# The first half of an output projection spread over six attention heads, and their probabilities turned by VectorE and a DRAM round

## The reference

```
u = rmsnorm(h, norm_g[l])
p = u @ w_in[l]                       # 1024 -> 9216 columns
hq, hf_f, hf_b, hi, hgt, aq, ak, av, agt = split(p)
o_h = hgrn2_mixer(...)                # 8 heads, gated linear recurrence in both directions
o_a = diff_attention_mixer(...)       # 8 heads
h = h + concat(o_h, o_a) @ w_out[l]   # 2048 -> 1024
```

```
s = einsum('bqhcd,bkhcd->bhcqk', q, k) * scale     # c = 0, 1: the two components, 64 wide
p = softmax(s)
p_diff = p[:, :, 0] - lam * p[:, :, 1]
o = einsum('bhqk,bkhv->bqhv', p_diff, v)           # v is 128 wide
o = rmsnorm(o, subln_g) * (1 - lam_init) * silu(gate)
```

## Time and profile before

| | |
|---|---|
| three runs, median | 1385.91 us |
| the profiled execution, its own time | 1386.22 us |
| its span | 1384.4 us |
| PE busy | 1369.9 us, 99% |
| DVE busy | 1046.2 us, 76% |
| ACT busy | 837.3 us, 60% |
| POOL busy | 186.0 us, 13% |
| DMA, share of 16 engines | 33.0% |
| granted TensorE clock | 9 tenths or more in all 40 slices |

### The profile page before, as it was taken

How to read it: one execution, slowest core, us unless ns; L and a number is a source line. 1 busy time by engine, 2 the same in 40 slices (tenths; PEclk the granted TensorE clock), 3 DMA queues, 4 the chain that set the end, 5 groups by cost and what they waited for, 6 DMA issues and landing times.

```text
span 1384.4 us, 32303 instructions
## 1 busy us (share of the span) xinstructions
PE 1369.9 (99%) x13108; PEld 1291.0 (93%) x13108; DVE 1046.2 (76%) x1765; ACT 837.3 (60%) x1802; POOL 186.0 (13%) x158
## 2 busy tenths in 40 slices
PE   9999999999999999999999999999999999999998
PEld 9999999998999999999998888888888899999987
DVE  6888887788646777877667888888886478888864
ACT  7666666666434666666555667666664456666654
POOL 1111222220000000000001122222210000000100
PEclk9999999999999999999999999999999999999999
DMA  5332322332323333333233232333323233334432
GB/s 188 117 98 93 108 85 86 108 108 78 99 71 122 101 99 100 103 90 100 70 107 108 87 106 85 108 107 108 108 82 108 85 110 107 108 107 114 114 96 76
DMA packets 76340, 140.41 MB, mean 101 GB/s; under 512 B 9504, under 2 KB 39456, under 8 KB 76192
## 3 DMA queue, kind: packets, MB, share of 16 engines
q1 hardware_dynamic: 76192, 138.35, 33.0%
HBM read 112.36 MB, written 17.30 MB: 94 GB/s over the span
## 4 chain that ended last, share of the span: by engine, by line
PE 89%; DVE 5%; ACT 2%; issue 2%; DMA 0%; SPq 0%; DVEq 0%; ACTq 0%
PE proj L1926 64%; PE far L2191 5%; PE pair L2174 3%; PE pair L2176 3%; PE far L2208 2%; PE pair L2059 1%; PE far L2193 1%; PE far L2144 1%; PE far L2145 1%; PE pair L2124 1%; DVE ops L1660 1%; PE pair L1926 1%; PE pair L2131 1%; DVE w_lo L1392 1%; PE far L2148 1%
## 5 line engine op out<-in xcount | busy, mean ns | idle before, releaser
L1926 PE MATMUL proj<-u_hi,w_hi 128*128 128x264 f32 (+1 forms) x1960 | 478.7, 312 | 1.9 <-DVE w_lo L1392 0.7
L1926 PE MATMUL proj<-u_lo,w_hi 128*128 128x264 f32 (+1 forms) x1960 | 458.2, 302 | 0.0
L1926 PE MATMUL proj<-u_hi,w_lo 128*128 128x264 f32 (+1 forms) x1960 | 458.1, 302 | 0.0
L1926 PEld LDWEIGHTS proj<-u_hi,w_hi 128*128 128x128 f32 x1960 | 314.7, 189 | 19.3 <-issue 1.4
L1926 PEld LDWEIGHTS proj<-u_hi,w_lo 128*128 128x128 f32 x1960 | 314.0, 188 | 13.6
L1926 PEld LDWEIGHTS proj<-u_lo,w_hi 128*128 128x128 f32 x1960 | 314.0, 188 | 10.6
L1392 DVE TENSOR_TENSOR w_lo<-w_raw,w_hi 128x1024 fp32r<-128x1024 f32 x178 | 221.9, 1247 | 35.9 <-ACT w_hi L952 35.8
L1200 ACT ACTIVATE decay<-pair,neg_max 128x528 f32<-128x528 f32 (+1 forms) x144 | 100.3, 697 | 203.4 <-DVE neg_max L1782 203.3
L952 ACT ACTIVATE w_hi<-w_raw 128x1024 fp32r<-128x1024 f32 x178 | 186.5, 1048 | 39.4 <-PE proj L1926 36.6
L1782 DVE TENSOR_REDUCE neg_max<-pair 128x1 f32<-128x528 f32 (+1 forms) x144 | 101.4, 704 | 90.5 <-PE pair L2176 89.3
L892 POOL TENSOR_TENSOR mix_lo<-mixed_t,mix_hi 128x528 fp32r<-128x528 f32 (+1 forms) x32 | 50.9, 1590 | 502.0 <-ACT mix_hi L1247 502.0
(11 more groups left out here) (257 smaller groups left out, 2245.7 us busy)
## 6 DMA issues: line engine op xcount, KB each, us to landing
w_raw<-w_units SPq DMA_DIRECT2D x178, 512.0 KB, 3.6
v_scratch<-blocks SPq DMA_DIRECT2D x128, 64.0 KB, 2.1
v_rows<-v_scratch SPq DMA_DIRECT2D x32, 256.0 KB, 2.9
o_scratch<-blocks SPq DMA_DIRECT2D x104, 64.0 KB, 2.7
q_stack<-gate_f SPq DMA_DIRECT2D x32, 132.0 KB, 2.4
k_stack<-k_stack SPq DMA_DIRECT2D x32, 132.0 KB, 2.4
o_rows<-o_scratch SPq DMA_DIRECT2D x14, 256.0 KB, 3.8
ops<-o_scratch SPq DMA_DIRECT2D x12, 256.0 KB, 2.6
```

The costliest lines, as they stand in the source:

```text
L1926: ins = pe.matmul(out, w, x[:, tile, cols_n], start=(k == 0 and p == 0), stop=(k == last_k and p == 2))
```

## The change

Six attention heads, 8 to 13 (`KEPT`), get part of the `outA` units: two are fed while head 8 is computed, one with heads 9 and 10 each, two with 11, one with 12 and one with 13. Their fed pieces are 41, 42, 41, 43, 42 and 43 (before: 96 and five times 32), because `CARRIED` lets the last few pieces of one head be fed in the next, and because the first four pieces of head 9's query unit are fed already in head 7 (`AHEAD`), which has 39 in place of 35. Since the slots of `mix_hi` are now free only after head 13, the six heads' gated outputs are kept in `ops` and split in head 14, steps 1 to 5 and 7.

In those six heads a chunk of 128 queries is no longer turned by TensorE, except for its 16 learned keys. At step 2j + 2, behind the difference, VectorE turns the 32 by 32 blocks into `p_blocks`; SP writes them to DRAM in four transfers at its step 2j + 3 and reads them back in one at 2j + 4; ACT copies from the landing buffer to `cols` at 2j + 5, and TensorE multiplies by the values at 2j + 6. The fifth chunk of 16 queries is still turned by TensorE, at step 11.

```
+KEPT = range(HG_HEADS, HEADS - 2)
+OUT_A_BEHIND = dict(zip((c + 1 for c in KEPT), (2, 1, 1, 2, 1, 1)))
-        if c == HG_HEADS + 1:
-            units += [("outA", c, j, c - 1) for j in range(OUT_TILES)]
+        for _ in range(OUT_A_BEHIND.get(c, 0)):
+            units.append(("outA", c, sum(u[0] == "outA" for u in units), c - 1))
...
+CARRIED = dict(zip(KEPT, (3, 1, 0, 5, 3, 0)))
 def carried(c):
-    return min(c + 1, 3) if c < HG_HEADS - 1 else 0
+    return min(c + 1, 3) if c < HG_HEADS - 1 else CARRIED.get(c, 0)
+AHEAD = 4
...
-    return left + own[:len(own) - carried(c)]
+    ahead = own_pieces(c + 1)[:AHEAD] if c == HG_HEADS - 1 else []
+    return left + own[AHEAD if c == HG_HEADS else 0:len(own) - carried(c)] + ahead
...
+def turn_step(c, j):
+    if not landed_from(c):
+        return 2 * j + 3
+    return 2 * j + 5 if j < N_CHUNKS else AT_STEPS - 2
+def value_step(c, j):
+    if not landed_from(c):
+        return 2 * j + 4
+    return 2 * j + 6 if j < N_CHUNKS else AT_STEPS - 1
...
 def split_turn(c, i):
-    return c == HG_HEADS or c > HG_HEADS + 1 and UNITS[i][0] == "ak"
+    return c == HG_HEADS or UNITS[i][0] == "ak"
...
+            def write_probs(b):
+                sp.wait_ge(p_blocked, b + 1)
+                if b >= 2:
+                    sp.wait_ge(p_landed, 16 * (b - 1))
+                for i in range(N_BLOCKS):
+                    sp.dma_start(p_scratch[b % 2][:, i, :].rearrange(...),
+                                 p_blocks[i * BLOCK:(i + 1) * BLOCK, :].rearrange(...)).then_inc(p_written, 16)
+            def read_probs(l, c, j):
+                b = block_of(l, c, j)
+                sp.wait_ge(p_written, 16 * N_BLOCKS * (b + 1))
...
+                sp.dma_start(p_landing[b % 2], p_scratch[b % 2].rearrange("p i x -> p (i x)")).then_inc(p_landed, 16)
...
                     dve.scalar_tensor_tensor(qk_dec[r, j % 2, 0, :], e1, row_inv[r, j % 4, 1:2], e0,
                                              ALU.mult, ALU.add).then_inc(p_ready, 1)
+                    if landed_from(c) and j < N_CHUNKS:
+                        b = block_of(l, c, j)
+                        dve.wait_ge(p_ready, chunks_before + j + 1)
+                        if b > 0:
+                            dve.wait_ge(p_written, 16 * N_BLOCKS * b)
+                        dve.transpose(p_blocks.rearrange(...), qk_dec[:, j % 2, 0, N_META:T].rearrange(...))
...
+                    act.wait_ge(p_landed, 16 * (b + 1))
+                    step(act.activation(cols[:, 0:4, :].rearrange(...), p_landing[b % 2].rearrange(...), ACT.Copy))
...
                 p = qk_dec[0:rows, j % 2, 0, :]
+                if not landed_from(c) or j == N_CHUNKS:
                     for kk in range(4):
                         pe.transpose(main[:, kk * P:kk * P + rows], p[:, chunk(kk)], ident[0:rows, 0:rows])
-                    pe.transpose(meta[0:N_META, 0:rows], p[:, 0:N_META], ident[0:rows, 0:rows])\
-                        .then_inc(p_turned, 1)
+                pe.transpose(turned_meta(c, j), p[:, 0:N_META], ident[0:rows, 0:rows]).then_inc(p_turned, 1)
...
+        def mixed_of(c):
+            return ops[:, (c - KEPT[0]) // 4, (c - KEPT[0]) % 4, :] if c in KEPT else mixed_t[:, :]
```

More of the change, by code:

```diff
@@ L1281, in _ @@
                                 stack_high(l, c + 1, i)
[L1282 to L1283 removed]
+                        for m in rounded(c, s):
+                            round_mixed(l, m)
                         for i in units_gated(c, s):
@@ L2195, in attend @@
[L2195 to L2206 removed]
+                for j in range(chunks):
+                    if s == value_step(c, j):
+                        times_values(l, c, j)
@@ new lines, in attend, with times_values @@
+                for j in range(chunks):
+                    if s == turn_step(c, j):
+                        turn_probs(l, c, j)
+            def times_values(l, c, j):
+                n, chunks_before = l * HEADS + c, before(l * AT_HEADS + c - HG_HEADS, 5, AT_HEADS)
+                pe.wait_ge(pt_ready, chunks_before + j + 1)
+                if j == 0:
+                    pe.wait_ge(v_landed, 16 * (n + 1))
+                out = attended(c, j)
+                for kk in range(4):
+                    pe.matmul(out, turned_probs(c, j, kk), v_main(kk), start=(kk == 0), stop=False)
+                pe.matmul(out, cols[:, meta_cols(c, j), :], v_meta[:, :],
+                          start=False, stop=True).then_inc(pv_done, 1)
```

206 lines of the change are left out of this document (125 added, 81 removed).

## The result

The changed kernel takes **1476.08 us** (median of four runs, 1475.38 to 1478.48) against 1386.11 before: a ratio of 1.0651 (95% interval 1.0636 to 1.0666), 90 us slower. I had forecast 1392.5, in a range of 1372 to 1405. The sign was right; the size was not, by 83.5 us.

What follows compares the result with a forecast made beforehand. PE's own work was taken to bound attention, with a ring through PE, DVE and ACT: -21.1 transposes, -3.9 head 7, +30.7 waits, +0.7 round, +6.4 on 1386.22; forecast 1392.5 us, own range 1385 to 1400, wider 1372 to 1405.

Steps and rivals of the forecast that it cites:

- the ring: Attention steps with scores: one scores buffer links PE, DVE and ACT, about 2.3 us a turn; new waits +30.7 us.
- What goes from PE: Heads 8 to 13, both layers: 48 chunks lose four transposes each, 0.43 to 0.44 us a chunk, -21.1 us.
- Head 7: Four pieces move from head 8 into head 7, three filling PE's idle time: net -3.9 us over both layers.
- DVE's new load: Heads 8 to 13: block transposes, splits and sums on DVE make PE wait for ACT's exponential, +30.7 us.
- the named steps: Forecast places of PE's waits: step 4 in heads 8 to 10, 6 in 8 and 11, 8 in 10 and 11.
- the bound of 40: Upper bound in us on DVE's new load, if each of some 25 waits also costs PE 0.3 us of restart.
- the terms given for layer one: PE's forecast waits in heads 8 to 13 of layer one, given as 15.9 us together.
- waits of 28 us: Upper end of the rival of slightly mis-sized waits, 22 to 28 us, giving 1383.1 to 1388.7 us; chance 17%.
- The rule that I weighed in the prediction: Skill's advice on 128 by 128 transposes, read as saying the six heads' turns should stay on TensorE; 0.43 against 0.65 us.
- The round: Probabilities through DRAM in heads 8 to 13: 6.0 to 7.2 us each, costing +0.7 us at layer two's last chunk.
- the landing late: Rival: rounds of 8.5 us or more make ACT wait at step 11 of each kept head; 1400 to 1412, 14%.

Runs made afterwards that it cites:

- e13: Changed kernel with stack transfers one step earlier and no DRAM round, DVE turning straight into the buffer ACT copies: 1409.71 us.
- e8: Changed kernel with SP's weight loads in heads 8 to 13 one step later and probability reads ahead of the stack transfers: 1418.72 us.
- e9: The outA spread alone (no DVE turning, no round), stack transfers one step earlier, nothing fed ahead in head 7: 1387.60 us.
- e5: The outA spread alone, four pieces fed ahead in head 7, next head's stack transfers one step earlier in SP's queue: 1394.65 us.
- e14: e8 with no piece of head 9 fed ahead in head 7: 1407.58 us.
- e12: Kernel before, all outA in head 8, with only head 8's probabilities turned by DVE and sent through DRAM on POOL's queue: 1382.79 us.
- e16: e12 with the probabilities' transfers on SP's queue in place of POOL's: 1382.49 us.
- e10: e8 with DVE turning only a quarter of each chunk, all transfers and waits kept: 1404.87 us.
- e1: Changed kernel with the outA spread and pieces ahead only; TensorE turns the chunks as before, no round: 1414.75 us.
- e4: Changed kernel with the probabilities' writes and reads issued from POOL's queue instead of SP's: 1468.39 us.
- e11: Changed kernel with probabilities' transfers on POOL's queue, two buffers for turned blocks and stack transfers one step earlier: 1459.70 us.

## Why the prediction was wrong, by its own steps

The runs make a chain from before to after. Most links change one thing; e13 and e8 differ also in where the stack transfers and the weight loads stand in SP's queue, and in the single buffer of turned blocks that DVE must wait for:

| step | from, to | measured | forecast |
|---|---|---|---|
| spread, nothing ahead | before, e9 | +1.3 | 0 |
| four pieces in head 7 | e9, e5 | +7.05 | -3.9 |
| DVE turns, PE does not | e5, e13 | +15.1 | -21.1 + 30.7 = +9.6 |
| the round, queue in order | e13, e8 | +9.0 | +0.7 |
| SP's order as in the change | e8, after | +57.4 | 0 |
| sum | | +89.8 | +6.4 |

The split depends on the order in which the steps are taken: with the round in place the four pieces cost 11.1 us (e8, e14). Of the 83.5 us, some 57 belong to the order of SP's queue and 8 to the rest of the round, 11 to head 7 and its pieces, 5.5 to the ring and 1.3 to the spread itself.

**What goes from PE: right.** 192 transposes, 0.44 us a chunk; e12 and e16 measure it cleanly, 1.8 us a layer for four chunks.

**Head 7: wrong in sign.** The step by which three of the four pieces fill idle time, because they stand ahead of the place at which PE waits, failed. I took DVE's load in head 7 as unchanged; its amount was, its order was not. The waits of PE in head 7 are for DVE and ACT, and the earlier pieces brought 2.5 us of DVE's work ahead of what PE waits for, 1.8 us of new waits over both layers. I also priced nothing for head 8, which loses the four pieces as cover: 3.8 us of waits for the exponential (e5 against e9). In the changed kernel head 8's first scores start at 350.44 where they started at 345.95: head 7 is some 4.5 us longer, and I had forecast 1.

**DVE's new load: right in mechanism, low in price.** The waits came at the named steps of heads 8 to 10 and were smaller than forecast in 11 to 13: 22.4 us for the exponential in the changed kernel, 26.5 of both kinds in e13. That the kernel is slower was no luck: e14, with queue and head 7 cured, still is, by 21 us. How much of the ring is DVE's turning and how much the cover that left PE with the transposes is shown in part only: with three quarters of the turning gone, 13.9 us come back (e10). I had left out what a wait costs beyond itself, although the bound of 40 named 0.3 us of restart for each: with clock and restarts the net is +15.1, not +9.6. That is 5.5 of the 83.5 us. (Two slips in the working change nothing: the terms given for layer one add up to 15.7 and not 15.9, and waits of 28 us give 1389.2 and not 1388.7.)

The rule that I weighed in the prediction (the Trainium skill, "VectorE: DVE Perf Modes", Rules for kernel authors: a 128 by 128 transpose on TensorE where PSUM will do) is borne out where `outA` is spread over the heads, by e14, +21 us. It is not for a head 8 that holds all of `outA`, by e12 and e16, -3.5 and -4.0 us: there PE is the bound and DVE has 40 us to spare.

**The round: the step that failed.** I had the two facts in the text and drew nothing from them: that "the last chunk's read stands behind a weight load that waits for DVE", and that weight loads are issued up to 2 us later, "so that costs nothing". The first I made a rival of, the landing late, at 1 to 2 us a head, 1400 to 1412 and 14%. Its sign and mechanism were right (in layer two it struck heads 9, 10, 11 and 13, where I had named 8 to 10 and 13) and its price several times too low: 6 to 7 us at a single product, and the clock behind it. I computed the round from durations (writes 1.74, read 3.4 behind, landing 2.6 to 3.8) as if the queue were empty when the read is due. From DVE's transpose to the landing I had 6.0 to 7.2 us; the median of the 48 chunks is 10.2 in the changed kernel and still 8.3 in e8. What counts is when the entry ahead of it is released: 1151.98, by a cut that DVE does at the end of its step. The second hid a consequence: the load is not late for its own user, but the stack transfers behind it are. They are in SP's queue too, and I did not price them in any of the heads. In e1 they cost 20 us without any round (e5). The term of 0.7 us for all of this stands against 9.0 for the round with the queue in order and 57.4 more for the queue's order.

The Trainium skill says this in "DMA: Bandwidth & Descriptors" (Anatomy of one DMA): DMA engines do not wait on semaphores, any wait happens on the issuing sequencer before dispatch. The trace agrees: between 1146.05 and 1151.98 SP issues nothing, while the DMA engines' share is 0.14 in the mean. The Trainium skill ("Trainium Kernel Development and Optimization", Key Constraints) says that issuing from several engines only saves the sequencer's issue time. Here it separated waits as well: in e4 PE's waits for ACT's copies fell from 44.7 to 25.5 us. But POOL's queue took most of the gain back, with up to 3.8 us from the start of the second write to that of the third (e11).

**The clock: left out.** No slice of the profile before showed a fall, and I had no term for it. Behind the four long waits it doubled the price of 2.9 to 5.7 us of work each time, some 8.5 us together (an estimate: half of that busy time).

## What to carry to other kernels

Price a transfer from the moment its queue entry can be reached, not from its own duration: list what stands ahead of it in the issuing engine's order and what semaphore each of these waits for, and do it for every transfer that the change moves past a waiting entry, also those it does not touch. A saving on an engine that is 99% busy is real only where the others have room in that very step: eight chunks moved off TensorE in a head that holds all of `outA` gave 3.5 to 4 us (e12, e16), while 48 in heads with `outA` spread over them cost 20 us more than they saved, even with the queue in order (e14 against e9). And idle time in front of a wait is filled by earlier work only if that work does not also bring other work of the awaited engine forward, and is not missed as cover where it was taken from.

## What the runs showed of the hardware that I had not expected

- The granted clock fell from 1.00 to 0.50 during PE's waits of 6.2 to 7.2 us at step 12 and stayed there for another 2.9 to 5.7 us of work; the same matmuls took 2.08 us in place of 1.05. In e8 a wait of 3.1 us was followed by a product of 2.08 us as well, in e1 one of 3.7 us was not (0.39 and then 0.28 for its matmuls, clock 1.00 in the six microseconds behind). It also fell with short waits alone: in e13 no wait of PE for the exponential or the copies is above 2.0 us, and the clock is at 0.50 in four stretches of 3.4 us.
- A row's start behind a wait is slower even at full clock: 0.39 us and 0.23 to the next, against 0.28 and 0.12; the value product takes 1.16 us in place of 1.05.
- Of the four writes of 64 KB that POOL issues for a chunk, the third starts 0.54 us behind the second where nothing holds it. In 26 of 48 chunks of e4 and 27 of e11 it starts over 1 us behind it, up to 3.1 and 3.8; in e12, with eight chunks, never. SP mostly issues four in 1.75 to 1.9 us.
- Two weight loads of 512 KB around the stack transfers held the 16 DMA engines at a share of 0.94 to 1.02 for six microseconds (e1, 396 to 402), and a stack transfer of 132 KB, with a median of 2.5 us, took over 4 to land.
